# A fused two-block transformer on one core: w_ada's tiles spread over the heads of the first attention, a later bias load, and the gate's product on VectorE

## The chip, the cores and the metric

One of the eight cores of a Trainium2 chip runs the whole program. The metric is device time in microseconds of one launch, the median of the runs shown. Lower is better. Inputs and outputs are float32 in device memory.

## The reference, cut to what matters

Two transformer blocks are applied to x (256 rows of 1024). Only the first half of the first block bears on this change:

```
mod = silu(c) @ w_ada + b_ada                  # w_ada is 1024 x 6144
sh1, sc1, g1, sh2, sc2, g2 = split(mod, 6)     # six chunks of 1024
h = rmsnorm(x, gain0) * (1 + sc1) + sh1
proj = h @ w_in                                # 1024 x 2304: q, k, v of 16 heads
out_a = attention, heads 0 to 7 (bias by distance, causal)
out_b = attention, heads 8 to 15 (window 128, bias by distance, a sink per head)
y = concat(out_a, out_b) @ w_out               # 1024 x 1024
x = x + g1 * rmsnorm(y, gain1)
h = rmsnorm(x, gain2) * (1 + sc2) + sh2
y = square(relu(h @ w1 + b1)) @ w2 + b2        # 4096 hidden
x = x + g2 * rmsnorm(y, gain3)
```

The second block (short convolution, spatial gating, two more attentions, gated feed-forward) follows and is the same in both kernels.

## The kernel before, in words

**Units and tiles.** Every weight matrix is cut into units of 128x1024 floats (512 KB). SyncE (SP) loads a unit into a raw tile, ScalarE rounds it to the high part wh (line 607, function round_static), VectorE subtracts to make the low part wl (line 975, low_static), and TensorE multiplies the activations' columns xT with both parts, three products per tile. Units 0 to 17 are w_in (U_PROJ1), 18 to 25 are w_out (U_OUT1), 26 and up are w1 (U_UP1). A unit's wh and wl lie in one of four slots, so that round_static(u) waits until TensorE is done with unit u-4.

**w_ada.** A tile i of w_ada (i = 0 to 39, eight each for the chunks sh1, sc1, g1, sh2, sc2) is not split. VectorE multiplies it by a column of silu(c) and adds it into ada_sum in one instruction (line 1082, function ada). TensorE sums ada_sum over the partitions later. Tiles 0 to 15 come before everything else; tiles 16 to 39 are mixed into the stream of w_in and w_out.

**The stream.** first_stream writes out the order of the first 66 loads by hand: unit u, then ada_after(u) tiles of w_ada. They share a ring of six raw tiles (FIRST_RING), in order: load number p waits until load p-6 has been consumed, by `low` for a unit and by `ada` for a tile of w_ada. Everything goes through SP's queue in program order, so that a wait holds back all behind it. After the units in BIAS_AFTER SP also issues eight loads of a half of the attention bias (dbias, line 425; heads 0 to 7, then 8 to 15). After unit 18 it loads the gain row for the gate into G1 (line 430). After unit 25 come small loads (line 440), then SP waits for all 40 tiles of w_ada to be consumed, and only then starts the loads of w1 (line 447).

**Projection.** Twelve units are multiplied (proj1_unit); meanwhile VectorE makes the low part of unit k+3 and takes one tile of w_ada after it. ScalarE rounds unit k+3 and moves banks out (leave_bank).

**The first attention.** Each engine then walks through slots i = 0 to 17. Head i's scores, softmax and transposes are spread over slots:

- TensorE: score(i) (lines 1550, 1555); in slots 0 to 3 the last projection units 12 to 17 (PROJ_SLOTS); from slot 5 on one half of a w_out unit (out1_half, lines 1410 to 1412, six matmuls); transpose_probs(i-1) (line 1378); in odd slots from 3 weigh_pair (lines 1591, 1593). Then come sums_to_rows (line 1485), out1_half of the last unit, and the transposes of the shift and scale sums.
- VectorE: score_head(i) (lines 1117 to 1121, scores plus bias, minimum), one tile of w_ada if any is left, the reciprocal of head i's sums (line 1142), the low part of the unit of SPLIT_SLOTS with more tiles of w_ada before it, in slots without a unit a second tile of w_ada, and in odd slots the split of the mixed columns (lines 983 and 984).
- ScalarE: round_static of the unit of SPLIT_SLOTS, exp_head(i) (line 755), scale_head(i) (lines 762, 763), leave_bank, copy_probsT(i-1) (line 771).

exp_head(i) waits for score_head(i); the reciprocal waits for exp_head(i); scale_head(i) waits for the reciprocal; transpose_probs(i) waits for scale_head(i) and for copy_probsT(i-1). Tiles of w_ada consumed in the attention of before, by slot (worked out from the code): slot 1: 26; 2: 27, 28; 3: 29, 30; 4: 31; 5: 32, 33; 7: 34, 35; 8: 36; 9: 37, 38; 10: 39. None comes in slots 11 to 17.

**The gate's product.** GpSimd (POOL) multiplies the eight summed tiles of g1 by the gain row in G1 (line 558), 128x1024 floats, as soon as both are there. TensorE's sums_to_rows waits for it (gain_scaled).

Of the kernel before, what the change touches and what calls it, by code (L numbers as in the profile page):

```python
# [29 lines left out]
D = 1024  # L30
KT = D // P
# [5 lines left out]
N_HEADS = 16  # L37
# [15 lines left out]
AHEAD = 3  # L53
# [32 lines left out]

def ada_after(u):

    return {5: 1, 6: 1, 7: 1, 8: 1, 9: 1, 10: 1, 11: 1, 12: 1, 13: 1, 14: 1, 15: 1, 16: 1, 17: 2, 18: 2, 19: 2, 20: 3, 21: 3}.get(u, 0)


def ada_units_after(u):
# [13 lines left out]
    return order  # L106


BIAS_AFTER = [5, 17]

STREAM = first_stream()
PLACE = {item: place for place, item in enumerate(STREAM)}
# [11 lines left out]

PROJ_SLOTS = {0: [12, 13], 1: [14], 2: [15, 16], 3: [17]}
OUT_SLOT = 5
SPLIT_SLOTS = {0: [15, 16], 1: [17], 2: [18], 4: [19], 6: [20], 8: [21], 10: [22], 12: [23], 14: [24], 16: [25], 17: [26]}


# [48 lines left out]
def build_program(nc, a):  # L178
# [25 lines left out]
    with ctx:  # L204
# [176 lines left out]
        def _(sp):  # L381
# [20 lines left out]
            for place, (kind, k) in enumerate(STREAM):  # L402
# [17 lines left out]
                if kind == "w" and k in BIAS_AFTER:  # L420
# [3 lines left out]
                    for g in range(P // COPIES):  # L424
# [1 line left out]
                                     bass.AP(tensor=bias_dram.tensor, offset=P - 1 - COPIES * g + N_MOBA * half * COPIES * DIST,  # L426
                                             ap=[[DIST - 1, COPIES], [COPIES * DIST, N_MOBA], [1, ROWS]]))\
                            .then_inc(bias_loaded[half], 16)
                if (kind, k) == ("w", U_OUT1):
                    sp.dma_start(G1[:, :], norm_gains[1].partition_broadcast(P)).then_inc(gain_loaded, 16)  # L430
                if (kind, k) == ("w", U_UP1 - 1):
                    for dst, src in [
# [60 lines left out]
        def _(pool):  # L493
# [58 lines left out]
            for r in range(RT):  # L552
                norm_rstd(N_IN1, r)

            pool.wait_ge(ada_used, (C_G1 + 1) * KT)
            pool.wait_ge(gain_loaded, 16)
            sums = ada_sum[:, D * C_G1:D * (C_G1 + 1)]
            nc.gpsimd.tensor_tensor(sums, sums, G1[:, :], ALU.mult).then_inc(gain_scaled, 1)
            for r in range(RT):
                norm_rstd(N_Y1, r)  # L560
                norm_rstd(N_FF1, r)
# [37 lines left out]
        def _(act):  # L599
# [9 lines left out]
            def round_static(u):  # L609
                if u < U_END:  # L610
                    r, count = raw_place(u)
                    full = (first_full if u < U_UP1 else raw_full)[r]
                    round_unit(full, raw_slot(r), 16 * count, u - RING + 1 if u >= RING else None, slot_of(u))
# [111 lines left out]
            def leave_bank(k):  # L725

                act.wait_ge(unit_done, k + 1)
                bank = acc[k % 4]
                if k < 4:
                    A(qT[:, k, :], bank[:, 0:ROWS], ACT.Copy, scale=SCALE).then_inc(acc_free, 1)  # L730
                elif k < 8:
                    A(kT[:, k - 4, :], bank[:, 0:ROWS], ACT.Copy).then_inc(acc_free, 1)
                elif k == 11:
                    A(vall[:, 0, 0:W_A], acc[0][:, :], ACT.Copy)
                    A(vall[:, 1, 0:W_A], acc[1][:, :], ACT.Copy).then_inc(acc_free, 1)
                elif 12 <= k < 16:
                    A(qT[:, k - 8, :], bank[:, 0:ROWS], ACT.Copy, scale=SCALE).then_inc(acc_free, 1)
                elif k == 16:
                    for kv in range(N_KV):
                        for half in range(2):  # L740
                            ins = A(kT[HD * half:HD * (half + 1), 4 + kv, :], bank[HD * kv:HD * (kv + 1), 0:ROWS], ACT.Copy)
                    ins.then_inc(acc_free, 1)
                elif k == 17:
                    A(vall[:, :, W_A:], bank[:, 0:ROWS].rearrange("p (r n) -> p r n", r=RT), ACT.Copy).then_inc(acc_free, 1)
# [28 lines left out]
            for k in range(11):  # L773
                round_static(k + AHEAD)
                leave_bank(k)
            leave_bank(11)
            round_static(11 + AHEAD)

            for i in range(N_HEADS + 2):
                for k in SPLIT_SLOTS.get(i, []):  # L780
                    round_static(k)
                if i < N_HEADS:
                    exp_head(i)
                if i < N_HEADS:
                    scale_head(i)
                for k in PROJ_SLOTS.get(i, []):
                    leave_bank(k)
                if 1 <= i <= N_HEADS:
                    copy_probsT(i - 1)
# [172 lines left out]
        def _(dve):  # L962
# [171 lines left out]
            for i in range(N_HEADS + 2):  # L1134
                if i < N_HEADS:
                    if i % N_MOBA == 0:
                        dve.wait_ge(bias_loaded[i // N_MOBA], 16 * P // COPIES)
                    score_head(i, dbias[:, i, :])
                    if ada_left:
                        ada(ada_left.pop(0))  # L1140
                    dve.wait_ge(exped, 2 * i + 2)
                    V.reciprocal(rsum[:, i, :], lsum[:, i, :]).then_inc(sums_inverted, 1)
                for k in SPLIT_SLOTS.get(i, []):
                    while len(ada_left) > 1:
                        ada(ada_left.pop(0))
                    low_static(k)
                    ada_left += ada_units_after(k)
                if i not in SPLIT_SLOTS and ada_left:
                    ada(ada_left.pop(0))
                if i >= 3 and i % 2 == 1:  # L1150
                    p = (i - 3) // 2
                    dve.wait_ge(pv_done, 2 * p + 2)
                    if p == 0:
                        dve.wait_ge(unit_done, U_OUT1)
                    split(xT[:, p, :], aux[3][:, 0:ROWS], mix_ready)

            dve.wait_ge(g_ready, 2)
            gated(N_Y1, 0, 0, G1)
# [709 lines left out]
```

## Time and profile before

| | |
|---|---|
| median of 3 runs | 781.82 us (781.82, 779.53, 782.61) |
| the profiled execution, its own time | 779.63 us |
| its span in the trace | 777.9 us |
| TensorE busy | 740.6 us, 95% of the span |
| VectorE busy | 514.2 us, 66% |
| ScalarE busy | 445.0 us, 57% |
| GpSimd busy | 40.0 us, 5% |
| granted TensorE clock | full in every slice |

The span is cut by the profiler at the first and last instruction; 1.7 us of the execution's own time lie around it. Times in the rows are from the start of the span. A row of a timeline gives the start, the duration, the engine, the line, what is written and read, and in square brackets the idle time before it with what ended it. The projection runs to about 73 us, the slots of the first attention from 73 to 142 us, and the first block's feed-forward starts at 160.7 us.

### The profile page before, as it was taken

How to read it: one execution, taken by the hardware profiler on the slowest of the kernel's cores; microseconds unless marked ns; L12 is line 12 of the kernel's file. 1: busy time of each engine (PE TensorE's matmuls, PEld its weight loads, DVE VectorE, ACT ScalarE, POOL GpSimd, SP SyncE). 2: the span in 40 equal slices, each digit the busy share in tenths (PEclk: the TensorE clock that was granted, in tenths of full speed). 3: DMA queues.
4: the chain of work that ended last, by engine and by line, in shares of the span. 5: the costliest groups of instructions: out<-in, count | busy, mean ns of one | idle time of the engine just before them, and what ended most of it. 6: DMA issues, size and time to landing. Idle time of an engine off the chain costs nothing.

```text
span 777.9 us, 12196 instructions
## 1 busy us (share of the span) xinstructions
PE 740.6 (95%) x4148; PEld 624.0 (80%) x4148; DVE 514.2 (66%) x746; ACT 445.0 (57%) x700; POOL 40.0 (5%) x70
## 2 busy tenths in 40 slices
PE   0699999999999999999999999999999999999998
PEld 0598966799999886777889777777788888888886
DVE  6887697788877743356657465665667777777443
ACT  0654678676666433355445687554546777776331
POOL 3000100100000100013110000000000000000000
PEclk9999999999999999999999999999999999999999
DMA  8999986257787655545764664544444666665651
GB/s 311 371 333 339 278 275 178 82 163 214 226 243 275 225 194 163 166 131 145 209 189 122 204 190 132 166 116 142 148 136 143 200 174 189 185 193 188 212 190 56
DMA packets 137423, 151.56 MB, mean 195 GB/s; under 512 B 6179, under 2 KB 111782, under 8 KB 137384
## 3 DMA queue, kind: packets, MB, share of 16 engines
q1 hardware_dynamic: 135566, 146.33, 60.1%
q10 hardware_dynamic: 1820, 4.74, 1.8%
q8 instruction: 23, 0.38, 0.2%
q14 instruction: 14, 0.11, 0.0%
HBM read 149.61 MB, written 1.44 MB: 194 GB/s over the span
## 4 chain that ended last, share of the span: by engine, by line
PE 48%; DVE 3%; issue 1%; ACT 1%; DVEq 0%; ACTq 0%
PE acc L1402 11%; PE acc L1410 9%; PE acc L1412 8%; PE acc L1411 8%; PE acc L1403 5%; PE acc L1390 1%; PE acc L1391 1%; PE acc L1389 1%; PE aux L1378 1%; DVE wl L975 1%; DVE rows_tmp L1266 1%; ACT wh L607 1%; DVE sig L1282 0%; DVE x_rows L1058 0%; PE aux L1581 0%
## 5 line engine op out<-in xcount | busy, mean ns | idle before, releaser
L975 DVE TENSOR_TENSOR wl<-raw,wh 128x1024 fp32r<-128x1024 f32 x217 | 266.2, 1232 | 151.6 <-ACT wh L607 150.7
L607 ACT ACTIVATE wh<-raw 128x1024 fp32r<-128x1024 f32 x217 | 228.0, 1055 | 124.9 <-PE acc L1412 112.8
L1389 PE MATMUL acc<-xT,wh 128*128 128x256 f32 x440 | 125.4, 285 | 3.3 <-DVE xT L1031 2.2
L1402 PE MATMUL acc<-xT,wh 128*128 128x512 f32 x352 | 124.5, 399 | 0.3 <-DVE xT L1013 0.3
L1390 PE MATMUL acc<-xT,wh 128*128 128x256 f32 x440 | 124.5, 283 | 0.0
L1391 PE MATMUL acc<-xT,wl 128*128 128x256 f32 x440 | 124.5, 283 | 0.0
L1410 PE MATMUL acc<-wh,xT 128*128 128x512 f32 (+1 forms) x272 | 108.6, 399 | 0.6 <-issue 0.3
L1412 PE MATMUL acc<-wh,xT 128*128 128x512 f32 (+1 forms) x272 | 104.4, 384 | 0.0
L1411 PE MATMUL acc<-wl,xT 128*128 128x512 f32 (+1 forms) x272 | 104.3, 384 | 0.0
L1403 PE MATMUL acc<-xT,wl 128*128 128x256 f32 x352 | 98.9, 281 | 0.0
L1389 PEld LDWEIGHTS acc<-xT,wh 128*128 128x128 f32 x440 | 84.4, 192 | 6.0 <-issue 2.6
L1410 PE MATMUL acc<-wh,hid 128*128 128x512 f32 x216 | 84.6, 392 | 0.0
L1390 PEld LDWEIGHTS acc<-xT,wh 128*128 128x128 f32 x440 | 84.4, 192 | 0.1
L1391 PEld LDWEIGHTS acc<-xT,wl 128*128 128x128 f32 x440 | 84.4, 192 | 0.0
L1411 PE MATMUL acc<-wl,hid 128*128 128x512 f32 x216 | 84.1, 389 | 0.0
L1412 PE MATMUL acc<-wh,hid 128*128 128x512 f32 x216 | 84.1, 389 | 0.0
L1402 PEld LDWEIGHTS acc<-xT,wh 128*128 128x128 f32 x352 | 66.1, 188 | 17.1 <-issue 0.7
L1403 PEld LDWEIGHTS acc<-xT,wl 128*128 128x128 f32 x352 | 66.5, 189 | 0.0
L1410 PEld LDWEIGHTS acc<-wh,xT 128*128 128x128 f32 x272 | 51.1, 188 | 17.0 <-issue 6.9
L1412 PEld LDWEIGHTS acc<-wh,xT 128*128 128x128 f32 x272 | 51.1, 188 | 10.5
L1411 PEld LDWEIGHTS acc<-wl,xT 128*128 128x128 f32 x272 | 51.2, 188 | 8.8 <-issue 0.2
L1410 PEld LDWEIGHTS acc<-wh,hid 128*128 128x128 f32 x216 | 40.5, 188 | 11.3 <-issue 3.0
(270 smaller groups left out, 894.6 us busy)
## 6 DMA issues: line engine op xcount, KB each, us to landing
raw<-in_w_in SPq DMA_DIRECT2D x66, 512.0 KB, 3.7
raw<-in_w SPq DMA_DIRECT2D x64, 512.0 KB, 4.3
raw<-in_w_ffn_in SPq DMA_DIRECT2D x44, 512.0 KB, 4.2
raw<-in_w_ada SPq DMA_DIRECT2D x27, 512.0 KB, 5.8
raw<-in_w_ffn_out SPq DMA_DIRECT2D x22, 512.0 KB, 4.3
raw_more<-in_w_ada SPq DMA_DIRECT2D x13, 512.0 KB, 6.5
raw<-in_w_out SPq DMA_DIRECT2D x13, 512.0 KB, 4.6
rows_tmp<-in_w_ada ACTq DMA_DIRECT2D x8, 512.0 KB
```

The lines of the kernel that those rows point to most:

```text
L607: A(wh[:, s, :], raw_unit, ACT.Copy).then_inc(rounded, 1)
L975: V.tensor_tensor(wl[:, s, :], raw_slot(r), wh[:, s, :].bitcast(f32), ALU.subtract).then_inc(split_ready, 1)
L1266: V.tensor_tensor(merged[:, r, :], merged[:, r, :], sig[:, r, :], ALU.add).then_inc(merged_ready, 2)
L1378: return mm(out, in_, ident[0:n, 0:n], start=True, stop=True, is_transpose=True)
L1389: mm(bank[:, 0:ROWS], wh[:, s, w], hi, start=(kt == 0), stop=False)
L1390: mm(bank[:, 0:ROWS], wh[:, s, w], lo, start=False, stop=False)
L1391: ins = mm(bank[:, 0:ROWS], wl[:, s, w], hi, start=False, stop=(kt == KT - 1))
L1402: mm(bank[:, :], wh[:, s, w], moving[:, kt, :], start=(kt == 0), stop=False, skip_group_check=True)
L1403: ins = mm(bank[:, 0:ROWS], wl[:, s, w], moving[:, kt, 0:ROWS], start=False, stop=(kt == KT - 1), skip_group_check=True)
L1410: mm(bank, hi, wh[:, s, cols], start=first, stop=False)
L1411: mm(bank, hi, wl[:, s, cols], start=False, stop=False)
L1412: return mm(bank, lo, wh[:, s, cols], start=False, stop=last)
```

## The change

Four things are changed, all in the first block.

1. The stream: ada_after is more even. Unit 17 is followed by one tile of w_ada, units 18 to 22 by two each, unit 23 by one. The second half of the bias is issued after unit 19 in place of 17, the gate's gain row after unit 23 in place of 18.
2. VectorE takes the last 14 tiles of w_ada (26 to 39) one per slot, in slots 1 to 14, always between score_head(i) and the reciprocal. The loops that took a second one are gone.
3. In slot 0 VectorE makes the low part of unit 15 between score_head(0) and the reciprocal; ScalarE runs round 15, exp_head(0), round 16 in that order (before: both rounds, then exp_head). Before the slots, ScalarE rounds unit 14 ahead of leave_bank(11) instead of behind it.
4. The gate's product is an instruction of VectorE at the end of slot 15, in place of GpSimd's.

```diff
-    return {5: 1, ..., 16: 1, 17: 2, 18: 2, 19: 2, 20: 3, 21: 3}.get(u, 0)
+    return {5: 1, ..., 16: 1, 17: 1, 18: 2, 19: 2, 20: 2, 21: 2, 22: 2, 23: 1}.get(u, 0)
-BIAS_AFTER = [5, 17]
+BIAS_AFTER = [5, 19]
+GAIN_AFTER = 23
+GAIN_SLOT = 15
+U_FIRST_SLOT = 15
-                if (kind, k) == ("w", U_OUT1):
+                if (kind, k) == ("w", GAIN_AFTER):
                     sp.dma_start(G1[:, :], ...).then_inc(gain_loaded, 16)
# GpSimd
-            pool.wait_ge(ada_used, (C_G1 + 1) * KT)
-            pool.wait_ge(gain_loaded, 16)
-            sums = ada_sum[:, D * C_G1:D * (C_G1 + 1)]
-            nc.gpsimd.tensor_tensor(sums, sums, G1[:, :], ALU.mult).then_inc(gain_scaled, 1)
# ScalarE
+            round_static(11 + AHEAD)
             leave_bank(11)
-            round_static(11 + AHEAD)
             for i in range(N_HEADS + 2):
+                if i == 0:
+                    round_static(U_FIRST_SLOT)
+                    exp_head(0)
                 for k in SPLIT_SLOTS.get(i, []):
-                    round_static(k)
-                if i < N_HEADS:
+                    if k != U_FIRST_SLOT:
+                        round_static(k)
+                if 0 < i < N_HEADS:
                     exp_head(i)
# VectorE
                     score_head(i, dbias[:, i, :])
-                    if ada_left:
-                        ada(ada_left.pop(0))
+                    if i == 0:
+                        low_static(U_FIRST_SLOT)
+                        ada_left += ada_units_after(U_FIRST_SLOT)
+                    else:
+                        if ada_left:
+                            ada(ada_left.pop(0))
                     dve.wait_ge(exped, 2 * i + 2)
                     V.reciprocal(rsum[:, i, :], lsum[:, i, :]).then_inc(sums_inverted, 1)
                 for k in SPLIT_SLOTS.get(i, []):
-                    while len(ada_left) > 1:
-                        ada(ada_left.pop(0))
-                    low_static(k)
-                    ada_left += ada_units_after(k)
-                if i not in SPLIT_SLOTS and ada_left:
-                    ada(ada_left.pop(0))
+                    if k != U_FIRST_SLOT:
+                        low_static(k)
+                        ada_left += ada_units_after(k)
...
+                if i == GAIN_SLOT:
+                    dve.wait_ge(ada_used, ADA_UNITS)
+                    dve.wait_ge(gain_loaded, 16)
+                    sums = ada_sum[:, D * C_G1:D * (C_G1 + 1)]
+                    V.tensor_tensor(sums, sums, G1[:, :], ALU.mult).then_inc(gain_scaled, 1)
```

## Rows read from the trace of the kernel before

**Rows 1.** The page's first part: busy time and share of each engine.
```profile
PE 740.6 (95%) x4148; PEld 624.0 (80%) x4148; DVE 514.2 (66%) x746; ACT 445.0 (57%) x700; POOL 40.0 (5%) x70
```

**Rows 2.** Busy time by stretch, slots 0 to 3: us, engines, clock, DMA share, GB/s.
```profile
78.00:84.00 6.00, 6.00 (x48) 5.54 (x47) 3.40 (x10) 5.50 (x13) 0.00 (x0) 1.00 1.08 232
84.00:92.00 8.00, 8.00 (x63) 7.33 (x63) 4.29 (x10) 3.71 (x12) 0.26 (x1) 1.00 1.04 364
92.00:99.00 7.00, 7.00 (x62) 6.30 (x61) 6.60 (x10) 5.02 (x16) 2.11 (x1) 1.00 0.57 204
```

**Rows 3.** Timeline of TensorE: weigh_pair of slot 3, transposes of heads 4, 6, ..., 14.
```profile
98.80 0.39 PE L1593 MATMUL aux<-probsT,vall 128*64 128x128 f32 x4
...
103.67 0.52 PE L1378 MATMUL aux<-ident,probs 128*128 128x128 f32 x3 [0.72 <-ACT probsT L771]
...
110.36 0.52 PE L1378 MATMUL aux<-ident,probs 128*128 128x128 f32 x3 [0.17 <-ACT probsT L771]
...
117.54 0.52 PE L1378 MATMUL aux<-ident,probs 128*128 128x128 f32 x3 [0.66 <-ACT probsT L771]
...
124.80 0.52 PE L1378 MATMUL aux<-ident,probs 128*128 128x128 f32 x3 [0.75 <-ACT probsT L771]
...
131.15 0.49 PE L1378 MATMUL aux<-ident,probs 128*128 128x128 f32 x3
...
137.47 0.49 PE L1378 MATMUL aux<-ident,probs 128*128 128x128 f32 x3
```

**Rows 4.** Timeline of VectorE, slots 3, 8, 9, 11 and 13.
```profile
98.30 1.28 DVE L1082 SCALAR_TENSOR_TENSOR ada_sum<-raw,cT,ada_sum 128x1024 f32<-128x1024 f32 x1
...
116.03 0.16 DVE L1142 RECIPROCAL rsum<-lsum 128x2 f32<-128x2 f32 x1
...
119.17 0.16 DVE L1142 RECIPROCAL rsum<-lsum 128x2 f32<-128x2 f32 x1
...
120.56 0.42 DVE L983 CAST xT<-aux 128x256 fp32r<-128x256 f32 x1
...
125.98 0.17 DVE L1142 RECIPROCAL rsum<-lsum 128x2 f32<-128x2 f32 x1 [0.67 <-ACT probs L755]
...
131.92 0.17 DVE L1142 RECIPROCAL rsum<-lsum 128x2 f32<-128x2 f32 x1 [0.67 <-ACT probs L755]
```

**Rows 5.** Timeline of ScalarE: round of unit 18, exp_head of heads 11 and 14.
```profile
90.41 1.06 ACT L607 ACTIVATE wh<-raw 128x1024 fp32r<-128x1024 f32 x1 [3.62 <-DMA raw<-in_w_out]
...
124.94 0.40 ACT L755 ACTIVATE probs<-logits,nmax 128x129 f32<-128x129 f32 x1 [0.29 <-DVE nmax L1119]
...
134.15 0.39 ACT L755 ACTIVATE probs<-logits,nmax 128x129 f32<-128x129 f32 x1
```

**Rows 6.** Timeline: GpSimd's product and the VectorE instruction beside it.
```profile
91.75 2.36 POOL L558 TENSOR_TENSOR ada_sum<-ada_sum,G 128x1024 f32<-128x1024 f32 x1 [69.45 <-DMA G<-in_norm_gains]
...
92.46 2.73 DVE L1082 SCALAR_TENSOR_TENSOR ada_sum<-raw_more,cT,ada_sum 128x1024 f32<-128x1024 f32 x1
```

**Rows 7.** Timeline of SP's queue: second half of the bias, first load of w1.
```profile
76.89 3.89 SPq L425 DMA_DIRECT2D dbias<-bias_by_distance  x8
...
124.74 49.11 SPq L447 DMA_DIRECT2D raw<-in_w  x11
```

**Rows 8.** DMA issues, us to landing: at 80.8 to 82 us, and at 124.5 to 130 us.
```profile
raw_more<-in_w_ada SPq DMA_DIRECT2D x1, 512.0 KB, 7.1
raw<-in_w SPq DMA_DIRECT2D x1, 512.0 KB, 4.6
```

**Rows 9.** Timeline: VectorE in slots 16 and 17, then TensorE's out1_half of the last unit.
```profile
140.32 1.23 DVE L975 TENSOR_TENSOR wl<-raw_more,wh 128x1024 fp32r<-128x1024 f32 x1 [0.61 <-ACT wh L607]
142.19 1.23 DVE L975 TENSOR_TENSOR wl<-raw,wh 128x1024 fp32r<-128x1024 f32 x1 [0.64 <-ACT wh L607]
143.33 0.42 DVE L983 CAST xT<-aux 128x256 fp32r<-128x256 f32 x1
...
144.26 0.76 PE L1410 MATMUL acc<-wh,xT 128*128 128x512 f32 x1
```

More of the change, by code:

```diff
@@ L87, in ada_after @@
 def ada_after(u):
-    return {5: 1, 6: 1, 7: 1, 8: 1, 9: 1, 10: 1, 11: 1, 12: 1, 13: 1, 14: 1, 15: 1, 16: 1, 17: 2, 18: 2, 19: 2, 20: 3, 21: 3}.get(u, 0)
+    return {5: 1, 6: 1, 7: 1, 8: 1, 9: 1, 10: 1, 11: 1, 12: 1, 13: 1, 14: 1, 15: 1, 16: 1, 17: 1, 18: 2, 19: 2, 20: 2, 21: 2, 22: 2, 23: 1}.get(u, 0)
 def ada_units_after(u):
@@ L1155, in _ @@
                     split(xT[:, p, :], aux[3][:, 0:ROWS], mix_ready)
+                if i == GAIN_SLOT:
+                    assert not ada_left
+                    dve.wait_ge(ada_used, ADA_UNITS)
+                    dve.wait_ge(gain_loaded, 16)
+                    sums = ada_sum[:, D * C_G1:D * (C_G1 + 1)]
+                    V.tensor_tensor(sums, sums, G1[:, :], ALU.mult).then_inc(gain_scaled, 1)
             dve.wait_ge(g_ready, 2)
```

## The prediction, as put on record before the kernel was run

> **What bounds the kernel now.** I read the page's busy shares first, then the busy time of each engine by stretch around the first attention, then the three engines' timelines there, the waits of SP's queue, and last where DMA loads land.
>
> The page says that TensorE is busy 95% of the span [rows 1]. So a change that touches VectorE, ScalarE and loads can gain only where TensorE stands still, and I looked for its holes between 60 and 160 us. In slots 0 to 3 there are none. TensorE is busy 6.00 of 6.00, 8.00 of 8.00 and 7.00 of 7.00 us [rows 2], with the projection's last six units. VectorE is busy only 3.40 and 4.29 us of the first two stretches, and ScalarE stands 3.62 us until unit 18 lands [rows 5]. These stalls are large, but TensorE doesn't notice them.
>
> From slot 4 on the reader should follow the transposes of the even heads [rows 3], at 103.67, 110.36, 117.54, 124.80, 131.15 and 137.47 us. The steps between them are 6.69, 7.18, 7.26, 6.35 and 6.32 us, each for two slots with the same work on TensorE. The last step has no hole in front of its transposes: 6.32 us is TensorE's own floor for a pair of slots. The first four transposes stand behind 0.72, 0.17, 0.66 and 0.75 us of idle time, ended by ScalarE's copy_probsT, and that comes in turn behind the reciprocal of VectorE. There VectorE has no idle time before its reciprocals (those of 116.03 and 119.17 us have no bracket), while those of 125.98 and 131.92 us stand behind 0.67 us of waiting [rows 4]. So the long steps are the slots in which VectorE takes up to three tiles of w_ada per pair, the short ones those in which it takes one or none. Above the floor the steps hold 0.37 + 0.86 + 0.94 + 0.03 = 2.20 us, and the 0.72 us before head 4's transposes come on top: about 2.9 us are all that can be won here.
>
> **The change part by part.**
>
> *Slot 0, the swap before it, and unit 18 earlier.* exp_head(0) no longer waits for unit 12 to leave its slot, unit 14 is rounded before ScalarE waits for unit 11, and unit 18's load waits for unit 15's low part, in slot 0, where before it waited for tile 26, in slot 1, behind the eight bias issues of 3.89 us [rows 7]. VectorE and ScalarE get earlier by several us in slots 0 to 2, the 3.62 us wait goes, and score_head(3) comes at once when its scores are there. The worth of it is zero, because TensorE's full queue covers it [rows 2]; if that cover were not real, it could be worth up to 3.62 us. What reaches slot 4 is only that VectorE isn't inside tile 30 when weigh_pair of slot 3 ends. In before that ends at 98.80 + 0.39 = 99.19 us [rows 3], and the tile holds VectorE from 98.30 for 1.2 us, until 99.5 [rows 4]. With the handshake, about 0.2 us are left: head 4's transposes come at 103.48, not 103.67 us. They still wait for one tile of w_ada (in slot 4 then as now).
>
> *The tiles, one per slot.* Every pair of slots up to 12 and 13 now has two. I price a pair by the loop that closes over VectorE and ScalarE. From exp_head of the even head to its reciprocal it takes 1.04 us when the reciprocal waits for it (124.94 to 125.98 us, a head without a tile [rows 4, 5]). From that reciprocal to the odd head's, with the low part, score_head and a tile between, 3.14 us (116.03 to 119.17 [rows 4]). From the odd head's reciprocal through scale, copy and round to the next exp_head, 2.23 us (131.92 to 134.15, with no bracket at the end: ScalarE is the one that is busy [rows 4, 5]). Together 6.41 us, a tenth above TensorE's floor. VectorE's own work is less: the pair of 7.26 us that it filled held three tiles, and the third cost 1.39 us (reciprocal 119.17 to cast 120.56 [rows 4]), which leaves 5.87 us. So the step in after is 6.41 us five times: 6.69, 7.18, 7.26, 6.35, 6.32 become 6.41 each, a saving of 0.28 + 0.77 + 0.85 - 0.06 - 0.09 = 1.75 us. With the 0.2 us before it, head 14's transposes come 1.95 us earlier. The bounds: the floor of 6.32 in every pair and no hole at head 4 give 2.9 us; a loop that stays as long as the longest now, 7.26 us, gives 36.3 against 33.8 us, a loss of 2.5 us.
>
> *The product on VectorE.* It is a float32 product of 128x1024, like the low part's 1.23 us [rows 9]; I take 1.2 us. In slots 16 and 17 VectorE now waits 0.61 and 0.64 us for the rounds [rows 9], so there is cover of 1.25 us in front of the last split, which then is the same distance from TensorE. But that split is already tight: cast at 143.33 us, 0.42 us plus its subtraction of the same size, and the matmul that needs it at 144.26 stands 0.76 us instead of some 0.5 [rows 9]. I charge 0.05 us. If the cover is gone, the product costs its 1.2 us in full. What is queued behind it on VectorE is the low part of units 25 and 26 and that split; TensorE's sums_to_rows waits for the product itself only about 2 us later. On GpSimd the product goes away: nothing is behind it there before 146 us.
>
> The tile of w_ada beside GpSimd's product took 2.73 us, against 1.28 for its like [rows 4, 6], so that 1.45 us of VectorE's time goes with it. It lies in slot 2 to 3, under TensorE's cover [rows 2], and counts zero.
>
> The Trainium skill ("SBUF — State Buffer", the reading notes on ports) says that VectorE and GpSimd share a port pair as an exclusive lock, and that a VectorE instruction with two SBUF inputs is blocked by a GpSimd one that reads SBUF. The trace agrees: GpSimd ran to 94.11 us, and the VectorE instruction ended 1.08 us after that. The skill's "Perfetto Trace Analysis" (Optimizing Scalar/DVE Operations) speaks against this edit: where VectorE is saturated, moving work to another engine, even GpSimd, may make sense. By that rule the product would cost its full 1.2 us on VectorE and the sum would be -0.7 instead of -1.9 us; by the rows VectorE is not saturated in slots 16 and 17.
>
> *Loads.* SP's ring keeps its six tiles. The bias of heads 8 to 15 is issued behind unit 19, once tile 27 is consumed, in slot 2, before 92 us [rows 2]. Its eight issues take 3.9 us and a load that stood behind them landed after 7.1 us [rows 7, 8], so it is there by 103 us, and the first head that needs it is 8, whose reciprocal is at 116.03 us [rows 4]: some 10 us early. The 3.9 us on SP's queue hold back tiles 31 and on, first needed in slot 6, some 7 us before that. The gain row is issued in slot 9 and used in slot 15. The one tight load is w1: SP waits for all 40 tiles, and the last now stands before head 14's reciprocal. A reciprocal lies 1.51 us before its transposes (116.03 to 117.54 [rows 3, 4]), so this is at 135.5 - 1.5 = 134.0 us at the latest, against 124.74 before [rows 7]. ScalarE's round of unit 26 is 1.06 us long [rows 5] and ended in before where the low part of 142.19 us begins [rows 9], so it began at 141.1 us and will want the unit at 139.2. A landing of 4.6 us makes it 138.6, in time; one of 7.1 us [rows 8] makes it 141.1 and costs 1.9 us.
>
> **Sum.** -0.2 - 1.75 + 0.05 = -1.9 us, against 779.63 us of the profiled execution, or 777.9 of span. Nothing behind 160 us changes. The profiled execution is 2.2 us below the median of 781.82; the four executions shown (781.82, 779.53, 782.61, 779.63) have a mean of 780.90. I take that mean as the level, since three runs leave the median open by an us: 780.9 - 1.9 = 779.0 us.
>
> **Rivals.**
> 1. *TensorE at its floor in every pair.* The loop of 6.41 us is made of pieces from different slots; if they overlap better, -2.9 us: 778.0. For it: VectorE's own 5.87 us leave 0.45 us to spare. Against: no long pair of now reaches the floor.
> 2. *The tail eats it.* The product or a late unit 26 pushes the last split, for it the tight cast at 143.33. Gives back 1.2 to 1.9 us: 780.5.
> 3. *The stalls of slots 0 to 3 were real.* If TensorE's busy share there hides waiting, the 3.62 us of unit 18 come on top: 775.4. Against it: matmuls of 6.00 in 6.00 us. This is the case of faster by over 0.5%.
> 4. *VectorE becomes the bound (slower).* Two tiles in each pair stretch the two pairs that ran at 6.35 and 6.32 us, and the others gain nothing. It decides when the loop of a pair is above the present mean, (137.47 - 103.67) / 5 = 6.76 us; at 7.26 it costs 2.5 us, and the product, then uncovered, 1.2: +3.7 us, 784.6. Against it: the reciprocals' 0.67 us of waiting in which a tile fits for 0.53 net.
>
> By the Trainium skill's rule on offloading, rival 2 is the one to expect.
>
> **How the numbers follow.** Forecast 0.47, rival 1 0.18, rival 2 0.20, rival 3 0.08, rival 4 0.07. Predicted 779.0 us. The range reaches from 777.0 (rival 1 with an us of the runs' scatter) to 782.2 (rival 2 with twice that), which leaves out rivals 3 and 4 and some scatter. No change that can be told is within 0.5%, 3.9 us: 777.9 to 785.7. The forecast and rivals 2 and 4 lie inside but for scatter; rival 1 lies at the edge. So faster 0.16, same 0.80, slower 0.04.
>
> **What would show it.** Right: even heads' transposes in after 6.3 to 6.5 us apart all along; no wait of 3.6 us for unit 18; no hole in slots 0 to 3 in either kernel; VectorE's product 1.2 us long, near 138 us; the last split's cast at about 141.4 us; the feed-forward's first matmul at 158.8, not 160.7 us. Wrong: steps of 7 us with two tiles; ScalarE waiting for a load of w1 near 139 us; the first transposes earlier than 103.2 us, which would mean that slots 0 to 3 had held something back.

## The result, and the profile after

| | before | after |
|---|---|---|
| median of 11 runs each | 781.02 us (779.53 to 783.32) | 776.69 us (774.38 to 778.38) |
| ratio, 95% interval | | 0.9941 (0.9926 to 0.9956) |
| own time and span of the profiled execution | 779.63, 777.9 us | 776.69, 775.0 us |

The forecast was 779.0 us (777.0 to 782.2). It came out 2.3 us lower, outside the range. Four sets of runs have both kernels side by side: these, and those of e1, e12 and e18 below. The means of before and after differ by 5.1, 4.1, 3.3 and 3.9 us there. Weighted by their errors that is 4.1 us, with a standard error of 0.26. The mean of before itself moved from set to set, between 779.1 (39 runs beside e13 to e16) and 781.4 us (the eleven above), so kernels are compared within one set of runs only.

The page's first part of after answers to [rows 1] and shows no difference that could explain it:

```profile
PE 739.6 (95%) x4148; PEld 624.9 (81%) x4148; DVE 513.4 (66%) x747; ACT 444.4 (57%) x700; POOL 39.8 (5%) x69
```

I measure the changed part as the **stretch** from the first matmul of unit 12 to the feed-forward's first matmul. These are the two rows of before's TensorE timeline, and the two of after:

```profile
74.30 0.39 PE L1389 MATMUL acc<-xT,wh 128*128 128x256 f32 x1 [0.39 <-ACT vall L735]
...
160.73 0.36 PE L1389 MATMUL acc<-xT,wh 128*128 128x256 f32 x1 [0.55 <-DVE xT L1023]
```
```profile
75.88 0.39 PE L1399 MATMUL acc<-xT,wh 128*128 128x256 f32 x1 [0.33 <-ACT vall L734]
...
105.16 0.52 PE L1388 MATMUL aux<-ident,probs 128*128 128x128 f32 x3 [0.62 <-ACT probsT L770]
...
111.52 0.49 PE L1388 MATMUL aux<-ident,probs 128*128 128x128 f32 x3
...
117.84 0.49 PE L1388 MATMUL aux<-ident,probs 128*128 128x128 f32 x3
...
124.17 0.49 PE L1388 MATMUL aux<-ident,probs 128*128 128x128 f32 x3
...
130.51 0.52 PE L1388 MATMUL aux<-ident,probs 128*128 128x128 f32 x3
...
136.88 0.52 PE L1388 MATMUL aux<-ident,probs 128*128 128x128 f32 x3
...
160.16 0.36 PE L1399 MATMUL acc<-xT,wh 128*128 128x256 f32 x1 [0.55 <-DVE xT L1026]
```

The stretch is 86.43 us in before and 84.28 in after: 2.15 us less, where 1.9 were forecast. Between the transposes of the even heads there are now 6.36, 6.32, 6.33, 6.34 and 6.37 us, with no hole in front of any but the first (before: [rows 3]). VectorE's timeline of after shows the same steps from the side of the reciprocals, and the product with the low parts and the last split behind it, which answer to [rows 4, 9]:

```profile
103.64 0.16 DVE L1149 RECIPROCAL rsum<-lsum 128x2 f32<-128x2 f32 x1
...
109.94 0.17 DVE L1149 RECIPROCAL rsum<-lsum 128x2 f32<-128x2 f32 x1 [0.42 <-ACT probs L754]
...
116.24 0.17 DVE L1149 RECIPROCAL rsum<-lsum 128x2 f32<-128x2 f32 x1 [0.36 <-ACT probs L754]
...
139.07 1.22 DVE L1165 TENSOR_TENSOR ada_sum<-ada_sum,G 128x1024 f32<-128x1024 f32 x1
140.42 1.23 DVE L978 TENSOR_TENSOR wl<-raw_more,wh 128x1024 fp32r<-128x1024 f32 x1
141.74 1.23 DVE L978 TENSOR_TENSOR wl<-raw,wh 128x1024 fp32r<-128x1024 f32 x1
142.88 0.42 DVE L986 CAST xT<-aux 128x256 fp32r<-128x256 f32 x1
```

VectorE waits 0.42 and 0.36 us before the reciprocals: with one tile per head it still has time left, and it isn't the bound. The product took 1.22 us and fills the place of two waits of before.

Outside the stretch the two profiled executions differ in two ways that the change doesn't touch, and both turned out to belong to single executions. Busy time of TensorE by stretch, with the granted clock, in after (us, busy, clock, DMA share, GB/s):

```profile
31.00:36.00 5.00, 4.67 (x18) 0.66 1.11 331
36.00:41.00 5.00, 3.59 (x24) 1.00 1.14 275
41.00:46.00 5.00, 4.83 (x28) 0.66 1.09 267
...
605.00:616.00 11.00, 11.00 (x66) 1.00 0.67 191
```

Twice in the projection the granted clock is at its lower level (1.2 GHz) for 3.4 us, and the stretch's start comes 1.58 us later than in before (75.88 against 74.30 us). And in the second block's feed-forward the loop over the gate and up matrices runs 66 matmuls in 11 us where before has 64 at the same clock of 1.00:

```profile
605.00:616.00 11.00, 11.00 (x64) 1.00 0.65 185
```

Over the eleven passes of the loop the difference is 2.3 us. So the profiled pair alone would tell a wrong story: 2.9 us of difference, which are 2.15 of the change and 2.3 of the loop's pace, less 1.6 lost before the stretch. What is beyond the 2.15 us in the timed runs had to be found otherwise.

### The profile page after: what moved, and what is told of

Same layout as the page of the kernel before. It is cut to its first block, busy times and chain, and to the rows that moved or that the text cites. A ratio compares the mean times of both kernels' runs of the same rounds, so it can differ in the third digit from the quotient of the medians.

```text
span 775.0 us, 12195 instructions
## 1 busy us (share of the span) xinstructions
PE 739.6 (95%) x4148; PEld 624.9 (81%) x4148; DVE 513.4 (66%) x747; ACT 444.4 (57%) x700; POOL 39.8 (5%) x69
## 4 chain that ended last, share of the span: by engine, by line
PE 48%; DVE 3%; issue 1%; ACT 1%; DVEq 0%; ACTq 0%
PE acc L1412 11%; PE acc L1420 9%; PE acc L1422 8%; PE acc L1421 8%; PE acc L1413 5%; PE acc L1400 1%; PE acc L1401 1%; PE acc L1399 1%; PE aux L1388 1%; DVE wl L978 1%; DVE rows_tmp L1276 1%; ACT wh L606 1%; DVE sig L1292 0%; DVE x_rows L1061 0%; PE aux L1591 0%
## 5 line engine op out<-in xcount | busy, mean ns | idle before, releaser
L1412 PE MATMUL acc<-xT,wh 128*128 128x512 f32 x352 | 122.2, 394 | 0.3 <-DVE xT L1016 0.3
```

Source lines behind the costliest of these rows:

```text
L1412: mm(bank[:, :], wh[:, s, w], moving[:, kt, :], start=(kt == 0), stop=False, skip_group_check=True)
```

## The experiments

Every ratio is against before in the same set of runs, on the same chip, with its 95% interval. "Stretch" is from the profiled execution of that kernel.

| run | what it is | ratio | stretch, us |
|---|---|---|---|
| e1, e12, e18 | after, verbatim | 0.9949 (0.9928 to 0.9971), 0.9951 (0.9931 to 0.9970), 0.9950 (0.9931 to 0.9969) | 84.27, 84.29, 84.30 |
| e2 | before, verbatim | 1.0004 (0.9979 to 1.0028) | 88.68 |
| e3 | tiles and stream only | 0.9955 (0.9931 to 0.9979) | 84.27 |
| e4, e17 | slot 0 only | 0.9981 (0.9954 to 1.0007), 0.9988 (0.9970 to 1.0005) | 86.33, 86.34 |
| e5 | product only | 1.0007 (0.9988 to 1.0025) | 86.35 |
| e6 | after, product on GpSimd | 0.9964 (0.9945 to 0.9984) | 85.36 |
| e7 | after, slot 4 without a tile | 0.9962 (0.9944 to 0.9980) | 83.85 |
| e8 | after, a third pass per pair | 0.9998 (0.9981 to 1.0014) | 87.69 |
| e9 | ada_after only | 0.9969 (0.9949 to 0.9989) | 85.98 |
| e10 | bias behind unit 19 only | 0.9989 (0.9973 to 1.0006) | 86.95 |
| e11 | e7, and round 19 in slot 3 | 0.9943 (0.9921 to 0.9964) | 83.83 |
| e13 | bias behind unit 18 only | 1.0036 (1.0016 to 1.0056) | 89.01 |
| e14 | gain row ahead of unit 18 | 1.0006 (0.9993 to 1.0020) | 87.78 |
| e15, e16 | before, verbatim | 1.0001 (0.9990 to 1.0013), e16 a single run without an interval | 87.36, 88.07 |

**The whole change and nothing, again (e1, e2).**

> The kernel after, unchanged. Of the 2.9 us by which the profiled span fell, 2.15 us lie between the projection's end and the first feed-forward (75.88 to 160.16 against 74.30 to 160.73 us) and 2.3 us in the second block's gate-and-up loop, whose passes take 11.10 us in place of 11.31; the projection itself gave 1.6 us back in a stretch of lower granted clock. If the loop's pace belongs to the program (theory placement), this run shows 11.10 us again and a ratio near 0.994. If it belongs to the single execution (theory chance), the pass may be 11.31 us here and the ratio near 0.997.

> The kernel before, unchanged, as the other half of the same test. Placement: 11.31 us a pass again and a ratio of 1.000. Chance: a pass of 11.10 us is as likely here.

The stretch of after came again to 0.01 us. That of before did not: 88.68 in place of 86.43 us, and I put the 2.25 us down to 6.8 us at the lower clock, which the records of e2 show there. It was half of the truth, as e15 and e16 showed later. e1's loop ran at the slow pace (11.31 us a pass, against 11.10 in the profiled after) with after's program, so the pace is not the change's work.

**One part at a time (e3, e4, e5).** e3 is before with the new ada_after and one tile per slot; e4 has only the edits of slot 0 and the swap before it, e5 only the product as an instruction of VectorE at the end of slot 15.

```diff
 e3, VectorE, besides ada_after:
-                    while len(ada_left) > 1:
-                        ada(ada_left.pop(0))
-                if i not in SPLIT_SLOTS and ada_left:
-                    ada(ada_left.pop(0))
```

> The kernel before with the new order of w_ada's tiles in the stream and one tile per slot; bias behind unit 17, gain row behind unit 18, product on GpSimd, slot 0 as before. My theory of the attention: this part holds nearly all of the 2.15 us, since the transposes of even heads come 6.4 us apart instead of up to 7.26; expected 1.7 to 2.0 us between the projection's last matmul and the feed-forward. Rival, the early stalls: it holds less than 1 us, and the parts of slot 0 hold the rest. The loop's pass: 11.31 us if only the program's layout in VectorE or ScalarE decides and it is close to the old one, open otherwise.

> The kernel before with the edits of slot 0 alone (unit 15's low part before the reciprocal, exp_head(0) before round 16, round 14 before leave_bank(11)); stream, tiles, bias and product as before. My theory: VectorE and ScalarE get earlier in slots 0 to 2 and TensorE doesn't notice, 0 to 0.3 us, ratio 1.000. Rival, the early stalls were real: 1 us or more.

> The kernel before with the gate's product on VectorE at the end of slot 15 and nothing else. My theory: from unit 12's first matmul to the feed-forward's it takes 86.4 to 86.6 us, as before (86.43), since VectorE waits 1.25 us for two rounds behind the product's place; the 1.45 us saved beside GpSimd's product lie under TensorE. Rival, the product is uncovered: 87.6 us. The second block's loop shows 11.31 or 11.09 us a pass, whichever the execution fell into.

The tiles carry all of the traced gain: 86.43 to 84.27 us in e3. Slot 0 is worth 0.10 us in its trace and the product 0.08. But e4's timed runs stood 1.5 us below before, more than its trace can explain, though with an interval that takes in zero. And e3's stood 3.6 us below (standard error 0.6), where its trace explains 2.2.

**The product's place, and a tile less or more (e6, e7, e8).** e6 is after with GpSimd's product back. e7 takes slot 4's tile into slot 3, behind its reciprocal. e8 puts one more multiplication of 128x1024, into a buffer that nothing reads then, behind the reciprocals of slots 5, 7, 9, 11 and 13; it adds work and leaves none out.

```diff
 e7, VectorE:
-                    else:
+                    elif i != 4:
                         if ada_left:
                             ada(ada_left.pop(0))
                     ...
+                if i == 3:
+                    ada(ada_left.pop(0))
 e8, VectorE, behind the reciprocal:
+                    if 5 <= i <= 13 and i % 2 == 1:
+                        V.tensor_tensor(val_all[:, 0:D], x[:, 0, :], x[:, 1, :], ALU.mult)
```

> The kernel after with the product back on GpSimd; the gain row is still loaded after unit 23, so the product runs near 127 us, beside the heads. Theory, the lock: one VectorE instruction of this stretch gets some 1.4 us longer, and here it is not covered, since the loop over VectorE and ScalarE sets the steps: 84.28 us from unit 12 to the feed-forward becomes 85 to 85.7. Rival, no cost: 84.1 to 84.3 us, the product's 1.2 us on VectorE given back.

> The kernel after with tile 29 taken in slot 3, behind the reciprocal, where VectorE now waits 4.55 us, and none in slot 4. If the loop that closes over both engines sets the pace from head 4 on, head 4's reciprocal comes 0.4 us earlier and all behind it too: 83.9 us from unit 12 to the feed-forward, against 84.28. If TensorE's floor sets it, 84.2 us.

> The kernel after with one more 128x1024 VectorE instruction (a product of two halves of x into a buffer that nobody reads) in each of the slots 5, 7, 9, 11 and 13. VectorE then has three such per pair of slots in all pairs, as before had in its longest. Theory, VectorE's count per pair sets the step: five steps of 7.2 to 7.26 us, 88.4 to 88.6 us from unit 12 to the feed-forward (84.28 + 5 x 0.85). Rival, the steps of before came from the waits and loads and not from the count: under 86.5 us.

The timelines of GpSimd and VectorE in e6 show the product and the tile beside it:

```profile
125.12 2.40 POOL L561 TENSOR_TENSOR ada_sum<-ada_sum,G 128x1024 f32<-128x1024 f32 x1 [101.32 <-DMA G<-in_norm_gains]
```
```profile
122.99 1.28 DVE L1089 SCALAR_TENSOR_TENSOR ada_sum<-raw_more,cT,ada_sum 128x1024 f32<-128x1024 f32 x1
...
125.78 2.81 DVE L1089 SCALAR_TENSOR_TENSOR ada_sum<-raw,cT,ada_sum 128x1024 f32<-128x1024 f32 x1
```

The tile takes 2.81 us in place of 1.28, and here, among the heads, 1.08 us of the 1.53 reach TensorE: the stretch is 85.36. The Trainium skill's "SBUF — State Buffer" (reading notes on ports: VectorE and GpSimd share a port pair as an exclusive lock) is borne out a second time. e7 gains the 0.43 us of head 4's hole. e8 shows what two tiles per pair leave free: five instructions of 1.2 us cost 3.41 us in all, 0.68 each. That is neither of its two forecasts. The stretch of 87.69 us is below the 88.4 to 88.6 of the theory that the count alone sets the step, and above the rival's 86.5. So the count of VectorE's instructions sets part of the step, and not all of it.

**The stream's two edits apart (e9, e10), and two more (e11, e12).**

> The kernel before with the new ada_after and its own loops on VectorE, so that slots still take two tiles where they have them. It separates the stream from the one-per-slot rule. Theory for the attention: the count per pair of slots decides, and the new stream by itself already hands out about two tiles per pair, so 84.3 to 84.9 us from unit 12 to the feed-forward; if the rule of one per slot is what matters, above 85.5 us. On the timed runs: outside this stretch the kernels with the new stream took 692.3 us on average (61 runs) and those with the old one 693.5 (92 runs). If the stream carries that, this one lies near 692.3.

> The kernel before with the second half of the bias issued after unit 19 in place of 17 and nothing else. Unit 18 then waits 3.9 us less in SP's queue, and ScalarE's wait of 3.62 us for it should go, with VectorE earlier by up to 4 us in slots 2 and 3. Theory, TensorE's queue covers it: 86.2 to 86.45 us from unit 12 to the feed-forward (86.43 before). Rival, late loads fed the holes of the attention: under 85.5 us.

> A version that should beat both: the kernel after with tile 29 in slot 3 (83.85 us from unit 12 to the feed-forward against 84.28), and ScalarE's round of unit 19 moved from slot 4 to slot 3, behind scale_head(3), where it waits 2.5 us. Then copy_probsT(2) goes before exp_head(4) alone. Expected 83.8 us: exp_head(4) was within 0.1 us of its scores already. Rival, the 0.19 us hole at head 4 and the steps behind it close: 83.4 to 83.6 us.

> The kernel after, unchanged, once more, on the same chip as the other three. From unit 12 to the feed-forward 84.28 us again. The second block's loop takes 11.09 or 11.31 us a pass: so far 11.09 in three of six profiled executions of kernels with the new stream and in none of four with the old one. If this is chance by execution, e9 to e12 show both values without regard to the kernel.

Both forecasts were missed. With ada_after alone the stretch falls by 0.45 us, to 85.98, and not to 84.3 to 84.9, so one tile per slot matters, and not only how many come per pair. With the bias behind unit 19 alone it rises by 0.52, to 86.95 where at most 86.45 was forecast, because head 5's reciprocal comes 0.5 us late: its tile waits 0.51 us for a load that the bias issues now hold back. Neither edit gains by itself what both gain with one tile per slot. e11's stretch is e7's, 83.83 against 83.85 us: the early round of unit 19 bought nothing. The slow pace of the loop showed in all four, with the clock at its lower level in the projection in three of them (not in e9) and the way from the start to unit 12 up to 3.0 us longer (e11 against e9): pace and clock change with the execution, not together.

**What the profiled execution of before did not show (e13 to e16).** By now the timed runs of before, less its traced stretch of 86.43 us, had a mean 1.3 us above those of the kernels with another order of loads, less theirs. The difference was there in the runs at a full clock too: before reached 695.0 us, the others 693.5. I read the traces of before (the profiled one and e2) and of e5 again, for anything that varied, and found the time at which ScalarE's round of unit 18 begins [rows 5].

```diff
 e13:
-BIAS_AFTER = [5, 17]
+BIAS_AFTER = [5, 18]
 e14:
-                if (kind, k) == ("w", U_OUT1):
+                if (kind, k) == ("w", U_OUT1 - 1):
                     sp.dma_start(G1[:, :], norm_gains[1]...)
```

> Kernel before with the second half of the bias issued behind unit 18 in place of 17. Theory (late unit 18): before's executions differ in when ScalarE's round of unit 18 begins, counted from unit 12's first matmul: 16.11 us in the profiled before, 16.84 in the product alone, 17.49 in before traced again; head 3's reciprocal follows 7.7 us later and its transposes another 1.79, while TensorE reaches them at 25.66. So each us beyond some 16.1 is a hole in TensorE there, though slots 0 to 3 show none in the profiled before. Without the eight issues ahead of it the round begins at 14.9 or earlier, the transposes of head 3 always at 25.66. The profiled stretch is 86.3 to 86.95 us (a tile may come late as with the bias behind unit 19). Timed runs, less the stretch: 692.5 as in the kernels with another stream (before: 693.8 in 101 runs); runs at a full clock none above 693.6. Rival (chance, or a state of the whole execution that goes with nothing here): 693.8, and full-clock runs up to 695.

> Kernel before with the gate's gain row (128x1024, one DMA) issued ahead of unit 18's load in place of behind it. Theory (late unit 18): unit 18 shares the queues with the bias and now with the row too; its round begins at 17 to 19 us from unit 12's first matmul, and head 3's transposes come as much later than 25.66 as the round is later than 16.1: 1 to 2.5 us of a hole in TensorE in slot 4, most of it left at the end of the stretch, 87.2 to 88.7 us at a full clock. Timed 1.001 to 1.003 of before. Rival (slots 0 to 3 are covered, as the prediction had it): the stretch stays at 86.4, timed 1.000.

> Kernel before, verbatim. Theory (late unit 18): the round of unit 18 begins anywhere from 16 to 18 us, head 3's transposes by as much beyond 25.66 as the round is beyond 16.1, the stretch 86.4 plus most of that. Rival (landing fixed, two of two traces of before differed by a half clock only): transposes at 25.66, stretch 86.43 at a full clock.

> Kernel before, verbatim, for a fourth trace. As for the third look: by the theory the landing of unit 18 differs again by some tenths to an us and the transposes of head 3 with it; by the rival they stand at 25.66.

First the profiled before, by its timelines: VectorE's reciprocal of head 3, then TensorE's transposes of that head.

```profile
98.12 0.15 DVE L1142 RECIPROCAL rsum<-lsum 128x2 f32<-128x2 f32 x1
```
```profile
99.96 0.55 PE L1378 MATMUL aux<-ident,probs 128*128 128x128 f32 x3
```

There is no bracket, so TensorE did not wait. The same in e16, which is the same kernel: round of unit 18 (ScalarE), reciprocal of head 3 (VectorE), the start of the stretch and the transposes (TensorE).

```profile
92.44 1.06 ACT L607 ACTIVATE wh<-raw 128x1024 fp32r<-128x1024 f32 x1 [5.22 <-DMA raw<-in_w_out]
```
```profile
100.17 0.15 DVE L1142 RECIPROCAL rsum<-lsum 128x2 f32<-128x2 f32 x1
```
```profile
74.73 0.39 PE L1389 MATMUL acc<-xT,wh 128*128 128x256 f32 x1 [0.39 <-ACT vall L735]
...
101.95 0.52 PE L1378 MATMUL aux<-ident,probs 128*128 128x128 f32 x3 [1.48 <-ACT probsT L771]
```

Now ScalarE waits 5.22 us for unit 18 in place of 3.62, and TensorE has a hole of 1.48 us. From reciprocal to transposes it takes 1.78 us where TensorE waits (101.95 - 100.17). In the profiled execution it was 1.84 us (99.96 - 98.12). The cover had 0.06 us left. The four traced executions of before, counted from unit 12's first matmul:

| | round of unit 18 | transposes of head 3 | stretch |
|---|---|---|---|
| profiled before | 16.11 | 25.66 | 86.43 |
| e15 | 17.00 | 26.50 | 87.36 |
| e2 | 17.49 | 26.99 | 88.68 |
| e16 | 17.71 | 27.22 | 88.07 |

Head 3 is late by what the round is late, less 0.05 us. In e2 and e16 the granted clock fell to its lower level 0.6 and 2.1 us behind the hole of head 3, for 6.8 and 3.4 us; in e15 it didn't. These are TensorE's windows of e16 (busy, granted clock):

```profile
99.00:103.00 4.00, 2.52 (x19) 1.00 0.70 200
103.00:107.00 4.00, 3.87 (x13) 0.62 0.98 365
107.00:111.00 4.00, 4.00 (x24) 0.95 0.91 305
```

The mean stretch of the four is 87.64 us, 3.35 us above after's 84.28. Four traces that scatter like these leave their mean uncertain by 0.5 us. The timed runs say 4.1 us with a standard error of 0.26. In all four traces of after the round of unit 18 begins at 10.67 or 10.68 us, with no wait:

```profile
86.17 0.49 ACT L770 ACTIVATE probsT<-aux 128x384 f32<-128x384 f32 x1
86.56 1.05 ACT L606 ACTIVATE wh<-raw_more 128x1024 fp32r<-128x1024 f32 x1
```

e14 makes unit 18 later still. Its round begins at 18.88 us, TensorE waits in slots 3, 4 and 5, and the stretch is 87.78, inside the forecast. The timed ratio of 1.0006 lies just below the forecast 1.001 to 1.003; before is late itself in three of its four traces. These are its transposes of heads 2, 3 and 4:

```profile
98.86 0.52 PE L1378 MATMUL aux<-ident,probs 128*128 128x128 f32 x3 [0.47 <-ACT probsT L771]
101.56 0.52 PE L1378 MATMUL aux<-ident,probs 128*128 128x128 f32 x3 [0.53 <-ACT probsT L771]
105.34 0.52 PE L1378 MATMUL aux<-ident,probs 128*128 128x128 f32 x3 [0.82 <-ACT probsT L771]
```

One part of e14's forecast failed, and it tells more than what came true. The round was 2.77 us later than in the profiled before, but head 3's transposes only 1.26 us (101.56 - 74.64 = 26.92 us from unit 12's first matmul). The reason is what stands between the two on VectorE. In before the tile of w_ada beside GpSimd's product takes 2.73 us [rows 6]. In e14 the gain row comes earlier, the product is over before that tile starts, and the tile takes 1.28 us. The same holds in e5, which has no product on GpSimd. First that tile in e14, then in e5:

```profile
95.57 1.28 DVE L1082 SCALAR_TENSOR_TENSOR ada_sum<-raw_more,cT,ada_sum 128x1024 f32<-128x1024 f32 x1
```
```profile
94.10 1.28 DVE L1078 SCALAR_TENSOR_TENSOR ada_sum<-raw_more,cT,ada_sum 128x1024 f32<-128x1024 f32 x1
```

From the round of unit 18 to head 3's reciprocal it takes 7.71 us in before and 6.26 us in both of these. TensorE needs that reciprocal by 23.88 us (25.66 less the 1.78). What is left until then, all counted from unit 12's first matmul:

| | round of unit 18 | reciprocal of head 3 | cover left |
|---|---|---|---|
| profiled before | 16.11 | 23.82 | 0.06 |
| e5, product only | 16.84 | 23.10 | 0.78 |
| e9, ada_after only | 16.20 | 22.79 | 1.09 |
| e4, e17, slot 0 only | 14.87, 14.60 | 22.60, 22.33 | 1.28, 1.55 |
| e3, tiles and stream | 15.59 | 22.17 | 1.71 |
| after | 10.68 | 20.25 | 3.63 |

So in the traces each part of the change widens the cover by itself, and not only slot 0. e4 and e17 have an earlier round, e3 and e9 one VectorE instruction less between round and reciprocal, and e5 a shorter one.

e13 was half a miss. As expected the round of unit 18 moved forward (15.02 us) and head 3's transposes stood at 25.67. But I had expected the kernel to be faster, and it was 0.36% slower: now the bias stood in front of unit 19, whose round began at 28.2 us in place of 25.36. Its rows, ScalarE's round of unit 19 and the transposes of head 4:

```profile
104.40 1.06 ACT L607 ACTIVATE wh<-raw 128x1024 fp32r<-128x1024 f32 x1 [2.73 <-DMA raw<-in_w_out]
```
```profile
107.89 0.52 PE L1378 MATMUL aux<-ident,probs 128*128 128x128 f32 x3 [2.30 <-ACT probsT L771]
```

It is the same mechanism one unit later, in a place without cover. The test that e13 was made for, its timed runs less its stretch, did not decide: they have 692.9 us, nearer to the theory's 692.5 than to the rival's 693.8, but before on the same chip, less 86.43, has 692.7 there and not 693.8.

**Slot 0 again (e17, e18).**

> The slot 0 edits alone, again. Theory (late unit 18): unit 18's load is issued 2.1 us earlier than in before (8.88 against 10.95 us from unit 12's first matmul), its round begins about a us earlier (14.87 in the first trace) and varies by an us or so, so that head 3's transposes stand at 25.66 us in nearly every execution: the stretch 86.33 traced, and timed runs 0.9 to 1.2 us below before, 0.9985 to 0.9988, which is what before loses on average by the late unit (its four traced executions: 0, 0.8, 1.3 and 1.6 us at head 3). Rival (slot 0 worth its traced 0.1 us): timed 0.9999, and both runs of this kernel together no different from before.

> Kernel after, verbatim, on the same chip. Theory: unit 18's round at 10.67 us, transposes of head 3 at 25.66, stretch 84.28; timed 3.0 to 3.5 us below before, 0.9955 to 0.9961 (2.15 of the stretch and the 1 us that before loses on average to the late unit). Rival (what is beyond the traced stretch was chance): 2.2 us, 0.9972.

e17's round of unit 18 begins at 14.60 us, the transposes of head 3 at 25.67. The timed means of e4 and e17 are 1.55 and 1.10 us below before in their own sets of runs, together 1.3 us with a standard error of 0.4. Each of the two intervals alone takes in zero. The slot 0 edits alone thus take away about what the late unit costs. e18 was 3.9 us faster than before on its chip, a little more than the 3.0 to 3.5 expected, inside its interval.

**Timed and traced side by side.** If before loses time to the late unit in most executions, then every kernel's timed mean should differ from before's by as much as its stretch differs from 87.64 us, and not from 86.43. For e3, e4, e6 to e11, e14 and e17 the two agree within 0.5 us, which is the error of one such timing. Two kernels do not fit. e5 should gain 1.3 us and gained 0.0 (standard error 0.5), though its trace shows more cover than before's. e13 should lose 1.4 us and lost 2.8 (0.5). Both have one trace only.

## Why the prediction was wrong, point by point

- **The holes of slots 4 to 13: right.** The steps were forecast at 6.41 us and are 6.32 to 6.37, against 6.69, 7.18 and 7.26 in the three long ones of before. The loop through VectorE and ScalarE was priced 0.06 us too long, because pieces from different slots overlap a little better. The traced gain is 2.15 us for 1.9: the steps give 2.08 for the 1.75 forecast, head 4 gives 0.09 for 0.2, and the tail loses 0.02 for 0.05. Rival 1 (the floor everywhere, 2.9 us) fell: head 4's hole stayed, 0.62 us, and e7 priced its removal at 0.43.
- **The product: right where it now stands.** It cost nothing there (e5: 86.35 against 86.43 us), and rival 2 fell. On GpSimd, among the heads, it would cost 1.08 us (e6). The prediction gave half of what the Trainium skill's "Perfetto Trace Analysis" (Optimizing Scalar/DVE Operations) says: the same paragraph warns that offloading between VectorE and GpSimd may not help, since they share a port, and e6 agrees with that half. The place that it left, slots 2 to 3, was priced wrongly; the point on slot 0 below says how.
- **w1: right.** The first load was issued 59.5 us behind unit 12's first matmul (135.36 - 75.88), where the estimate comes to 59.7 (134.0 - 74.30). VectorE began its low part at 65.86 us on that count (141.74), 2.0 us earlier than before (142.19 [rows 9]).
- **Rival 4 fell**, with room: a third pass in each pair costs 0.68 us of its 1.2 (e8).
- **Slot 0: the failed step.** "The worth of it is zero, because TensorE's full queue covers it [rows 2]". The row was true, for that execution. A busy share of 7.00 in 7.00 us says that nothing waited; it doesn't say how much later the covered thing may come. The cover had 0.06 us left, and what it covered was a DMA that lands anywhere within 1.6 us from one execution to the next. The four traces of before put the average cost at 1.2 us, e4 with e17 at 1.3 (standard error 0.4). The same step stands a second time in the prediction: the 1.45 us that the tile loses beside GpSimd's product "lies in slot 2 to 3, under TensorE's cover [rows 2], and counts zero". It lies in the chain from unit 18 to head 3, and without it the cover would have been 1.5 us and not 0.06. Rival 3 named the mechanism, but priced it as all or nothing (3.62 us) and gave it 0.08. The sign that the prediction set for it, transposes earlier than 103.2 us, did not come, because it compares with the one execution of before that was not late.
- **The level: not the cause of the miss.** I took 780.9 us, and the eleven runs of before beside this result have a median of 781.02 and a mean of 781.4. The gain was too small: 1.9 us forecast, 4.3 between the medians. I laid the range's low end at rival 1 with one us of scatter, and left out that scatter and an unseen cost could add.
- **The sum.** 1.9 us, with 0.25 more in the stretch and 1.2 of the late unit, is 3.35 us. The four sets of runs have 4.1 us (standard error 0.26). The 0.75 us between them are not explained; the two errors together (0.5 for the mean of four traces, 0.26 for the timed runs) come to 0.55.
- **"Nothing behind 160 us changes": right.** From the feed-forward's first matmul to the second block's loop every one of the 20 traces has 429.4 or 429.5 us. The loop's two paces are found in both kernels: the fast one in 3 of 10 traces with before's order of tiles and in 3 of 10 with after's.

Open: why head 3's lateness is followed by the lower clock in two of three executions, what sets the loop's pace, and why e5, whose trace has the wider cover, was no faster than before. That unit 18 comes late and delays head 3 is shown by four traces of before and by e14; that this is all of what the timed runs show beyond the trace is not shown.

## What to carry to other kernels

A resource that is busy all through a stretch hides a wait only by its slack: take the time from the waiting chain's last link to the instruction that needs it, subtract what that link takes where it does wait, and put the difference beside the scatter of the DMA at the chain's head. If the slack is smaller than that scatter, the edit that brings the load forward has a worth, even when the profile of one execution shows no hole. Bulk issues (here eight for a bias) belong behind loads whose consumer has slack; each place in the queue has to be read for the unit that comes next. What stands in the chain between the load and the instruction that needs it counts too: a VectorE instruction that takes 2.73 us in place of 1.28 is free only while the slack is larger.

## What the runs showed of the hardware that was not expected

- The gap between matmuls of the same program has two values, one per execution. Two pairs of matmuls in the second block's loop, first in after, then in before, both at a granted clock of 1.00:

```profile
604.65 0.40 PE L1412 MATMUL acc<-xT,wh 128*128 128x512 f32 x1
...
605.34 0.40 PE L1412 MATMUL acc<-xT,wh 128*128 128x512 f32 x1
```
```profile
604.79 0.40 PE L1402 MATMUL acc<-xT,wh 128*128 128x512 f32 x1
...
605.49 0.40 PE L1402 MATMUL acc<-xT,wh 128*128 128x512 f32 x1
```

  A pair takes 0.347 us in one and 0.354 in the other on average over the loop, 11.10 or 11.31 us a pass, 2.3 us per execution. Of before's four traces two have the fast pace, of after's four one.
- The same load, behind the same eight issues, ended ScalarE's wait after 3.62, 4.51, 5.02 and 5.22 us in four executions of one kernel.
- A GpSimd product of 2.40 us lengthened the VectorE instruction beside it from 1.28 to 2.81 us.
